# Down stage of a mixture layer: from column 46 on, one product of 512 per high chunk, a ScalarE copy and a VectorE add in place of two products of 256

## The reference, cut to what matters

```python
u = w_down[eidx]                                    # [tokens, 8, 16, 1024]
a = gelu(einsum('btd,btpkd->btpk', hblk, u))
vv = w_up[eidx]
return einsum('btpk,btpkd->btd', w * a, vv)
```

## Time and profile before

| | |
|---|---|
| median of 3 runs | 1203.29 us (1199.77 to 1206.89) |
| profiled execution, its time | 1205.66 us |
| its span, first to last instruction | 1203.9 us |
| mean granted TensorE clock | 0.989 of full speed |
| PE / DVE / ACT / POOL busy, share of the span | 95% / 74% / 51% / 60% |
| down stage, first to last product | 475.0 to 871.4 us |
| up stage and end | 873.5 to 1203.9 us |

### The profile page before, as it was taken

One profiled execution on the slowest core, in us unless ns is written; L12 is line 12 of the kernel. 1 busy time (PEld: TensorE's weight loads), 2 busy tenths in 40 slices (PEclk: granted clock), 3 DMA queues, 4 the chain that ended last, 5 costly groups with the idle time before them and its releaser, 6 DMA issues.

```text
span 1203.9 us, 18849 instructions
## 1 busy us (share of the span) xinstructions
PE 1141.1 (95%) x6904; PEld 987.6 (82%) x6904; DVE 886.1 (74%) x1762; ACT 617.4 (51%) x1186; POOL 719.5 (60%) x451
## 2 busy tenths in 40 slices
PE   4999999999998999999999999999999999899995
PEld 2778877777776799999999999999977767677884
DVE  5678666587878652999665666666588889898886
ACT  1545444453554444445565656555564545455563
POOL 0886759674443202888777777798665766465600
PEclk9999999999999999999999999999999999999998
DMA  9988774445341441565555555576579999999975
GB/s 375 420 328 338 278 293 161 184 166 207 143 158 71 177 173 36 186 194 196 188 168 184 169 176 184 176 260 193 177 248 347 357 331 333 340 346 342 351 265 156
DMA packets 68332, 282.06 MB, mean 234 GB/s; under 512 B 10384, under 2 KB 10768, under 8 KB 55952
## 3 DMA queue, kind: packets, MB, share of 16 engines
q1 hardware_dynamic: 56544, 246.54, 57.6%
q0 software_dynamic: 11264, 33.60, 7.6%
q10 hardware_dynamic: 432, 0.72, 0.2%
HBM read 274.53 MB, written 6.29 MB: 233 GB/s over the span
## 4 chain that ended last, share of the span: by engine, by line
PE 70%; DVE 11%; DMA 9%; issue 4%; ACT 3%; POOL 2%; SPq 0%; DVEq 0%; POOLq 0%; ACTq 0%
PE bank L1649 10%; PE bank L1653 10%; PE bank L1650 10%; DMA ring<-in_up 8%; PE banks L1243 3%; PE banks L1249 2%; PE bank L1243 2%; PE bank L1249 2%; PE bank L1255 2%; PE banks L1255 2%; DVE banks L2315 2%; PE banks L1663 2%; DVE split_r L2328 2%; PE banks L1702 1%; PE bank L1697 1%
## 5 line engine op out<-in xcount | busy, mean ns | idle before, releaser
L845 POOL TENSOR_TENSOR split_r<-ring,split_r 128x1024 fp32r<-128x1024 f32 x128 | 307.9, 2406 | 137.2 <-ACT split_r L911 137.1
L911 ACT ACTIVATE split_r<-ring 128x1024 fp32r<-128x1024 f32 x192 | 203.3, 1059 | 232.1 <-PE bank L1653 171.8
L1649 PE MATMUL bank<-h_high_r,split_r 128*128 128x256 f32 x1024 | 251.4, 283 | 0.7 <-issue 0.7
L1650 PE MATMUL bank<-h_low_r,split_r 128*128 128x256 f32 x1024 | 251.2, 283 | 0.0
L1649 PEld LDWEIGHTS bank<-h_high_r,split_r 128*128 128x128 f32 x1024 | 196.5, 192 | 0.9 <-ACT G L1081 0.9
L1650 PEld LDWEIGHTS bank<-h_low_r,split_r 128*128 128x128 f32 x1024 | 196.5, 192 | 0.0
L798 POOL TENSOR_TENSOR wq_low_r<-G,G_r 128x512 fp32r<-128x512 f32 (+1 forms) x104 | 134.9, 1331 | 48.5 <-ACT G_r L906 48.5
L829 POOL DMA_INDIRECT G<-in_up,tab x64 | 93.4, 1460 | 87.2 <-DVE banks L2315 71.6
L1653 PE MATMUL bank<-h_high_r,split_r 128*128 128x256 f32 x1024 | 143.7, 283 | 0.0
L1653 PEld LDWEIGHTS bank<-h_high_r,split_r 128*128 128x128 f32 x1024 | 132.1, 192 | 0.0
L798 POOL TENSOR_TENSOR wq_low_r<-G,hT_r 128x512 fp32r<-128x512 f32 x48 | 63.2, 1351 | 57.2 <-ACT hT_r L906 57.2
(11 more groups left out here) (477 smaller groups left out, 2581.2 us busy)
## 6 DMA issues: line engine op xcount, KB each, us to landing
ring<-in_down SPq DMA_DIRECT2D x128, 512.0 KB, 3.6
ring<-in_up SPq DMA_DIRECT2D x128, 512.0 KB, 5.7
G<-in_ada SPq DMA_DIRECT2D x32, 1024.0 KB, 10.6
G<-in_in SPq DMA_DIRECT2D x32, 1024.0 KB, 7.2
G<-in_out SPq DMA_DIRECT2D x8, 1024.0 KB, 7.1
G<-in_wq SPq DMA_DIRECT2D x8, 1024.0 KB, 7.8
z_few<-G SPq DMA_DIRECT2D x16, 256.0 KB, 2.2
tab<-in_ada SPq DMA_DIRECT2D x4, 1024.0 KB, 8.3
```

Source lines behind the costliest of these rows:

```text
L845: pool.tensor_tensor(wsplit[:, j % SPLIT, 1, :], raw[:, j % RAW, :], wsplit[:, j % SPLIT, 0, :].bitcast(F32), ALU.subtract).then_inc(low_r ...
L911: nc.scalar.activation(split_parts(n)[:, 0, :], raw[:, n % RAW, :], ACT.Copy).then_inc(high_ready, 1)
L1649: mm(o, w[0][:, c, :], h_high[:, c, :], start=(c == 0), stop=False)
L1650: mm(o, w[0][:, c, :], h_low[:, c, :], start=False, stop=False)
```

## The change

From column `JOINED` = 46 on (82 of the 128 columns) `down(j)` takes the high part of the weights once per chunk: `h_low` and `h_high` now lie side by side (`h_both`), and one product of 512 writes the low tokens' product to words 0 to 255 of the bank and the high tokens' to words 256 to 511. The 8 products with the low part of the weights go to words 256 to 511. Then ACT copies words 0 to 255 to SBUF (`z_low`), ahead of `expert_high`, and DVE adds them into words 256 to 511 in place (`join`), for which it waits. `gelu(j)` waits for this sum and reads it there. DVE's loop has a new order: `join(j)` first in each column, and `weigh_late(j)` last instead of first. Columns 0 to 45 are as before. `z_low` is one buffer; ACT waits for the earlier column's `join` before it writes it again.

```diff
--- before.py
+++ after.py
@@ -46,6 +46,7 @@
 K16 = 16
 RAW = 4
 SPLIT = 2
+JOINED = 46
 BATCH = 4
 FEW = 64
 TD = T - FEW
@@ -384,6 +385,7 @@
         tab = sb("tab", n_tab + 1024)
         keep = sb("keep", n_keep)
         small = sb("small", 744)
+        z_low = sb("z_low", T)[:, :]
 
 
         TMP = SLOTS * PANEL
@@ -397,7 +399,8 @@
         w_both_r = over("w_both_r", "x", D + 2 * T, 2 * T)
         hot_r = over("hot_r", "tab", 0, 6 * BATCH * P)
         split_r = over("split_r", "ring", RAW * D, 2 * SPLIT * D)
-        h_high_r, h_low_r = over("h_high_r", "rows", 0, C * T), over("h_low_r", "hT3", 0, C * T)
+        h_both_r = over("h_both_r", "hT3", 0, 2 * C * T)
+        h_low_r, h_high_r = h_both_r[:, 0:C * T], h_both_r[:, C * T:2 * C * T]
 
         def view(tensor, off, *dims):
             n = int(np.prod(dims))
@@ -520,6 +523,7 @@
         wsplit = view(split_r, 0, SPLIT, 2, D)
         h_high = view(h_high_r, 0, C, T)
         h_low = view(h_low_r, 0, C, T)
+        h_both = view(h_both_r, 0, 2, C, T)
         up_split = [wsplit[:, 0], wsplit[:, 1], view(h_high_r, 0, 2, D), view(h_low_r, 0, 2, D)]
         x_back, gfin2, fin = view(G, 0, NT, D), view(G, 2 * D, D), view(G, 4 * D, NT, D)
         Gv = view(G, 0, P, TD)
@@ -567,6 +571,7 @@
         few_named, few_weighed, row_used = sem("few_named"), sem("few_weighed"), sem("row_used")
         row_fetched = [sem(f"row_fetched{k}") for k in range(ROW_BUFFERS)]
         z_stored, z_taken = ([sem(f"{name}{k}") for k in range(2)] for name in ("z_stored", "z_taken"))
+        z_low_moved, z_joined = sem("z_low_moved"), sem("z_joined")
         few_moved, few_added, gate_added = sem("few_moved"), sem("few_added"), sem("gate_added")
         wq_high, wq_low, wq_done = sem("wq_high"), sem("wq_low"), sem("wq_done")
         x0_high_ready, x0_low_ready = sem("x0_high_ready"), sem("x0_low_ready")
@@ -1096,7 +1101,9 @@
 
             def gelu(j):
 
-                src, done, m = ps[j % 2][:, 0:T], with_weights(j), j // STAGE
+                src, done, m = ps[j % 2][:, 0:T] if j < JOINED else ps[j % 2][:, T:2 * T], with_weights(j), j // STAGE
+                if j >= JOINED:
+                    act.wait_ge(z_joined, j - JOINED + 1)
                 if done:
                     if with_weights(j - 1):
                         act.wait_ge(z_done, late_columns(j - 1))
@@ -1125,6 +1132,10 @@
             nc.scalar.activation(dummy[:, 3:4], ones[:, 0:1], ACT.Gelu_apprx_tanh)
             for j in range(P):
                 act.wait_ge(col_done, j + 1)
+                if j >= JOINED:
+                    if j > JOINED:
+                        act.wait_ge(z_joined, j - JOINED)
+                    nc.scalar.activation(z_low, ps[j % 2][:, 0:T], ACT.Copy).then_inc(z_low_moved, 1)
                 expert_high(j + SPLIT) if j + SPLIT < P else None
                 gelu(j)
                 if j == J0 - 2:
@@ -1644,13 +1655,16 @@
                 if j >= 2:
                     pe_.wait_ge(gelu_done, j - 1)
                 pe_.wait_ge(high_ready, j + 1)
-                o = ps[j % 2][:, 0:T]
+                o = ps[j % 2][:, 0:T] if j < JOINED else ps[j % 2][:, T:2 * T]
                 for c in range(C):
-                    mm(o, w[0][:, c, :], h_high[:, c, :], start=(c == 0), stop=False)
-                    mm(o, w[0][:, c, :], h_low[:, c, :], start=False, stop=False)
+                    if j < JOINED:
+                        mm(o, w[0][:, c, :], h_high[:, c, :], start=(c == 0), stop=False)
+                        mm(o, w[0][:, c, :], h_low[:, c, :], start=False, stop=False)
+                    else:
+                        mm(ps[j % 2][:, :], w[0][:, c, :], h_both[:, :, c, :], start=(c == 0), stop=False, skip_group_check=True)
                 pe_.wait_ge(low_ready, j + 1)
                 for c in range(C):
-                    ins = mm(o, w[1][:, c, :], h_high[:, c, :], start=False, stop=(c == C - 1))
+                    ins = mm(o, w[1][:, c, :], h_high[:, c, :], start=False, stop=(c == C - 1), skip_group_check=(j >= JOINED))
                 ins.then_inc(col_done, 1)
 
             def weights(m):
@@ -2286,17 +2300,26 @@
                 g = Gv[:, j, 0:with_weights(j)]
                 tt(g, zbuf[:, 0:with_weights(j)], g, ALU.mult).then_inc(z_done, 1)
 
+            def join(j):
+
+                dve.wait_ge(col_done, j + 1)
+                dve.wait_ge(z_low_moved, j - JOINED + 1)
+                z = ps[j % 2][:, T:2 * T]
+                tt(z, z, z_low, ALU.add).then_inc(z_joined, 1)
+
             for m in range(2):
                 build(m)
             for j in range(J0, P):
-                if with_weights(j):
-                    weigh_late(j)
+                if j >= JOINED:
+                    join(j)
                 if j in BATCH_COLUMN:
                     add_low(BATCH_COLUMN.index(j))
                 if j in KEEP_COLUMN:
                     weigh(KEEP_COLUMN.index(j))
                 if j in BATCH_COLUMN and BATCH_COLUMN.index(j) + 2 < NB:
                     build(BATCH_COLUMN.index(j) + 2)
+                if with_weights(j):
+                    weigh_late(j)
 
             def add_row(k):
 
```

## The result

The changed kernel takes 1232.01 us in the median of 4 runs (1224.42 to 1238.65), the kernel before 1205.09 beside it (4 runs). That is 27 and 23 us more; forecast were 26.4 more and 1229.7. Both intervals lie clear of 1; whether the loss is more or less than 2% they leave open. The profiled execution is the fastest of its four, with 1224.42 and a span of 1222.5.

The account below looks back on a forecast made before the run. PE was taken to bound the kernel before. Longer rounds from column 47 to 122 add 26.2, seven other columns -0.7, the stage's end +0.9: +26.4 on 1203.29 gives 1229.7 us, range 1211 to 1243.

Parts of the forecast that it names:

- PE bounds the stage, DVE is close behind: Kernel before, columns 47 to 122: PE busy 238.54 of 238.57 us; DVE close behind it at neighbouring batches.
- Part 1, products: PE's products from column 46: a column takes 2.778, 0.102 less; 8.3 us over 82 columns if PE stays the bound.
- Part 2, the copy: ACT's copy to `z_low` ahead of `expert_high`: record 0.387, turn 0.29; POOL's later start hidden from PE.
- Part 3, the circle: ACT, DVE, ACT loop through `join`, behind `build`, and gelu: two-column rounds 6.505 instead of 6.24, single ones 4.855 instead of 3.47.
- the sum: All terms added: +26.2 for columns 47 to 122, -0.7 for seven other columns, +0.9 at the stage's end: +26.4; chance 0.70.
- The moved weigh_late costs nothing by itself.: DVE's `weigh_late` moved to last: no cost, since the next column's gelu waits for `join`, later in the same queue.
- The end of the stage: Behind column 127, copy, hand-overs and add come before gelu, for which the up stage waits: +0.9.
- The up stage is as before: The stage after the changed one: no difference in its length.
- PE as the bound: Rival: DVE reaches `join` by the column's end, so PE still bounds the stage; -7.4, 1195.9; chance 0.08.
- Only neighbouring batches are late: Rival: two-column rounds fit into PE's 6.04, only one-column rounds lose; +12, 1215; chance 0.13.
- The round is longer: Rival: copy and add at upper bounds, +18, 1248; a third of the way or slower hand-overs, +7 to +13; chance 0.07.
- the rival of the clock: PE, busy about 88% of the stretch, drops to 1.2 GHz; a column takes 5.56, each 25 us costs 11; chance 0.02.

Follow-up runs that it names:

- wide_only: Changed kernel without the copy, the add and gelu's wait, DVE's order as before; low tokens' sum incomplete; 1200.24 against 1206.61 us for the kernel before, ratio 0.9953.
- wide_copy: As wide_only, with the copy to `z_low` back on ACT ahead of the high part, nothing reading it; ratio 0.9973 to the kernel before.
- join_twice: Changed kernel with a second add of the same size on DVE ahead of `join`; ratio 1.0354 to the kernel before.
- copy_twice: Changed kernel with a second copy, 128 wide, on ACT ahead of that to `z_low`; ratio 1.0252 to the kernel before.
- join_ahead: Changed kernel with DVE's next-column `join` ahead of `build` and `weigh_late` right behind `join`; 1204.93 against 1207.19 us for the kernel before, ratio 0.9984.
- late_first: Changed kernel with `weigh_late` right behind `join`, ahead of `add_low` and `build`, instead of last; ratio 1.0133 to the kernel before.
- order_only: Kernel before with one edit, `weigh_late` last in each DVE column, behind `build`; 1216.64 against 1206.61 us, ratio 1.0072.

## Why the prediction was right

By its own steps:

- *PE bounds the stage, DVE is close behind.* Right, and the row at the neighbouring batches was the one to look at: by the starts of `add_low` neighbours were 3.412 apart before and 4.833 after, 13 x 1.421 = 18.5 of the 24.8 us. The rounds of two columns, 6.265 before and 6.469 after, make the other 6.3.
- *Part 1, products.* Mis-sized by little: 2.795 per column instead of 2.778, so 0.085 instead of 0.102 less per column. The Trainium skill, "TensorE: Matmul & The Clock Gate", section "Back-to-back issue gap", would have given 1.5 us for the 75 columns of the stretch by its formula for an isolated product, N/2.4 + 2.5 ns. The trace does not agree: wide_only is 5.4 shorter, so the rows' price held.
- *Part 2, the copy.* The record is 0.405 in the median (0.387 taken), its turn 0.27 to 0.28 (0.29 forecast). POOL's record stayed at 2.40 and no wait of PE before L1667 shows in the list, so the low parts did not come late. But "hidden" holds for the low parts only: at neighbours it delays `weigh`, 0.27 each (wide_copy). In the changed kernel that is covered by the longer wait for `join`.
- *Part 3, the circle.* Right in place and size: 6.469 against 6.505, 4.833 against 4.855, together 263.4 against 264.8. With the stage's end the up stage begins 24.7 later; the sum said 26.4. Each term stands in the trace; join_twice and copy_twice change one term each and the rounds follow, and join_ahead opens the circle and the loss is gone.
- *"The moved weigh_late costs nothing by itself."* This sentence failed, and the prediction's own sum contradicts it. Inside the change the move costs 0.16 in every round, 6.9 us (late_first); the sum came out only because the 0.17 stood in the circle anyway. Alone it costs 8 us (order_only), since gelu waits for it through `z_done`.
- *The end of the stage:* +0.9 forecast, 3.04 - 2.09 = 0.95 measured.
- *The up stage is as before:* its length in one execution was 6 less, in another 1 less, within what executions of one kernel differ. What sets it apart from one execution to the next was not tried.
- *The rivals.* PE as the bound failed in the changed kernel; it comes back in join_ahead, but for PE's waits at neighbouring batches: DVE had the time, but not in the right place of its queue. "Only neighbouring batches are late" failed too, since the rounds of two columns took 6.469 and not 6.04. "The round is longer" did not come: the rounds were 0.02 to 0.04 shorter than the sum. (Its "third of the way" is a slip: a third of 18 is 6, not 7.) The clock stayed at 1.00 in the changed kernel, where PE was busy for 92% of the stretch and not 88%; PE's pauses were 8% of it, "a tenth or so" in the forecast.

## What to carry to other kernels

An engine that is idle a third of the time can still be the bound: ask where in its queue the new step stands, what long work of the same engine is in front, and whether a chain leads from its result back to the start of that work. Add up such a circle per round, for each kind of round, and compare it with the bound's own round; rounds that are longer are lost in full, and rounds that are shorter give nothing back beyond the bound. Then put what others wait for ahead of what nobody needs yet.

## What the runs showed of the hardware

In join_twice the granted clock fell for short stretches, busy time of each engine by tens of us:

```profile
800.00:810.00 10.00, 8.28 (x48) 7.00 (x47) 7.24 (x19) 5.23 (x17) 5.87 (x3) 1.00 0.53 162
...
820.00:830.00 10.00, 8.21 (x39) 6.72 (x39) 7.25 (x18) 5.20 (x17) 7.02 (x4) 0.85 0.60 207
```

With PE busy for 8.3 and 8.2 of 10 us it once kept 1.00 and once was granted 0.85. In order of time, PE around one of its long pauses:

```profile
844.02 0.64 PE L1677 MATMUL banks<-hot_r 128*128 128x256 f32 x4
846.43 2.91 PE L1664 MATMUL bank<-h_both_r,split_r 128*128 128x512 f32 x8 [1.77 <-ACT G L1115]
849.14 1.90 PE L1667 MATMUL bank<-h_both_r,split_r 128*128 128x256 f32 x8
850.85 2.02 PE L1664 MATMUL bank<-h_both_r,split_r 128*128 128x512 f32 x8
```

Behind a pause of 1.77 the eight products of 512 took 2.71 (846.43 to 849.14) instead of 1.84 and the eight of 256 took 1.71 (849.14 to 850.85) instead of 0.95; the next column was at full speed again. 0.214 a product is what the lower level of 1.2 GHz gives (256 columns in 0.213). The changed kernel, whose pauses reach 1.53 there, showed 1.00 over this stage, in both of its profiled executions. The pause alone does not decide: in join_twice the pauses of 1.75, 1.77 and 1.82 (ended at 826.50, 846.43 and 873.45) lie where the clock fell, but behind one of 1.71 (807.31) and one of 1.85 (893.52) it kept 1.00. So the rival of the clock may have been nearer than its 2% looked: 0.3 to 0.4 us more in each round was enough to see the clock fall, in the one execution of join_twice that was profiled.
